# Output stages of the second network's mixers: where and when the split weights of output tiles 4, 5 and 7 are made

## The reference, cut to what matters

```python
for i in range(4):                       # mixers: gdn0, hgrn, gla, gdn1
    m = mixer_i(x, ...)                  # ends in o.reshape(B, T, 1024) @ w_out
    x = layer_norm(DN_ALPHA * x + m, mix_ln_g[i], mix_ln_b[i])
    x = layer_norm(DN_ALPHA * x + swiglu(x, ffn_w_in[i], ffn_w_down[i]), ...)
```

## Time and profile before

| what | value |
|---|---|
| device time, median of three | 2551.23 us (2549.55 to 2552.09) |
| span of the profiled execution | 2545.7 us |
| PE busy | 2464.1 us, 97% |
| DVE busy | 1769.0 us, 69% |
| ACT busy | 1179.2 us, 46% |
| granted PE clock over the 40 slices | 9 tenths or more in each |

### The profile page before, as it was taken

The page is one execution under the profiler, slowest core; times in us unless marked ns, Lnnn a source line. Parts: engine busy times, 40 slices in busy tenths (PEclk is TensorE's granted clock), DMA queues, the critical chain, the costliest instruction groups (busy, mean ns, idle before and its releaser), DMA issues.

```text
span 2545.7 us, 46612 instructions
## 1 busy us (share of the span) xinstructions
PE 2464.1 (97%) x17610; PEld 2261.9 (89%) x17610; DVE 1769.0 (69%) x2863; ACT 1179.2 (46%) x1816; POOL 105.9 (4%) x161
## 2 busy tenths in 40 slices
PE   8999999999999999989999999999989999989998
PEld 6866777778798999988999998999989999988997
DVE  5878699988747866675665767666457657766665
ACT  4554421223545444455544544544545446455443
POOL 2221000000000000003000000000000000000000
PEclk9999999999999999999999999999999999999999
DMA  7323255554424554321555431555415554222553
GB/s 296 141 104 137 100 182 186 183 182 154 167 92 148 191 181 162 112 84 67 173 182 189 159 108 67 181 181 183 157 51 177 186 179 152 100 75 75 198 178 121
DMA packets 119641, 378.13 MB, mean 149 GB/s; under 512 B 11592, under 2 KB 29000, under 8 KB 119121
## 3 DMA queue, kind: packets, MB, share of 16 engines
q1 hardware_dynamic: 105936, 327.58, 38.1%
q0 software_dynamic: 12528, 47.62, 5.4%
q10 hardware_dynamic: 1040, 1.05, 0.1%
HBM read 375.15 MB, written 1.05 MB: 148 GB/s over the span
## 4 chain that ended last, share of the span: by engine, by line
PE 85%; DVE 9%; ACT 4%; issue 2%; DMA 0%; DVEq 0%; ACTq 0%; SPq 0%
PE gb L597 22%; PE gb L598 21%; PE gb L599 21%; DVE w_lo L566 3%; PE mb L676 2%; PE mb L2636 2%; PE gb L1162 1%; ACT w_hi L560 1%; PE gb L2617 1%; PE gb L2132 1%; PE mb L2150 1%; PE mb L599 1%; PE mb L598 1%; PE mb L597 1%; DVE W L2372 1%
## 5 line engine op out<-in xcount | busy, mean ns | idle before, releaser
L597 PE MATMUL gb<-Xs,w_hi 128*128 128x256 f32 (+1 forms) x3584 | 1098.3, 306 | 18.1 <-DVE w_lo L566 5.2
L599 PE MATMUL gb<-Xs,w_lo 128*128 128x256 f32 (+1 forms) x3584 | 1083.3, 302 | 0.0
L598 PE MATMUL gb<-Xs,w_hi 128*128 128x256 f32 (+1 forms) x3504 | 1053.4, 301 | 0.0
L560 ACT ACTIVATE w_hi<-raw 128x1024 fp32r<-128x1024 f32 x616 | 646.6, 1057 | 775.8 <-PE gb L599 730.6
L566 DVE TENSOR_TENSOR w_lo<-raw,w_hi 128x1024 fp32r<-128x1024 f32 x616 | 747.7, 1225 | 222.6 <-ACT w_hi L560 215.6
L597 PEld LDWEIGHTS gb<-Xs,w_hi 128*128 128x128 f32 x3584 | 679.0, 189 | 73.6 <-issue 29.9
L599 PEld LDWEIGHTS gb<-Xs,w_lo 128*128 128x128 f32 x3584 | 678.5, 189 | 31.2
L598 PEld LDWEIGHTS gb<-Xs,w_hi 128*128 128x128 f32 x3504 | 664.3, 190 | 26.4 <-issue 1.2
L598 PE MATMUL gb<-Fs,w_hi 128*128 128x256 f32 (+1 forms) x1016 | 294.4, 290 | 0.0
L597 PE MATMUL gb<-Fs,w_hi 128*128 128x256 f32 (+1 forms) x936 | 263.2, 281 | 0.0
L599 PE MATMUL gb<-Fs,w_lo 128*128 128x256 f32 (+1 forms) x936 | 261.9, 280 | 0.0
(11 more groups left out here) (402 smaller groups left out, 2889.9 us busy)
## 6 DMA issues: line engine op xcount, KB each, us to landing
raw<-in_up SPq DMA_DIRECT2D x264, 512.0 KB, 3.8
raw<-in_down SPq DMA_DIRECT2D x96, 512.0 KB, 3.6
R<-in_mod_later POOLq DMA_DIRECT2D x80, 512.0 KB, 3.9
raw<-in_gdn_in SPq DMA_DIRECT2D x64, 512.0 KB, 3.6
raw<-in_down SPq DMA_DIRECT2D x48, 384.0 KB, 3.9
raw<-in_hgrn_in SPq DMA_DIRECT2D x32, 512.0 KB, 3.9
raw<-in_ev_in SPq DMA_DIRECT2D x24, 512.0 KB, 5.3
raw<-in_gla_in SPq DMA_DIRECT2D x24, 512.0 KB, 4.1
```

The lines of the kernel that those rows point to most:

```text
L560: nc.scalar.activation(w_hi[:, slot], raw[:, slot], ACT.Identity).then_inc(*hi_ready.inc())
L597: nc.tensor.matmul(to, w_hi[:, w_slot, k, :], x_hi, start=start, stop=False)
L598: nc.tensor.matmul(to, w_hi[:, w_slot, k, :], x_lo, start=False, stop=False)
L599: return nc.tensor.matmul(to, w_lo[:, w_slot, k, :], x_hi, start=False, stop=stop)
```

## The change

Output tiles 4, 5 and 7 of the four stages get places of their own for their split weights. Tile 4's and 5's lie in columns T to 2T of `Xs` (eight rows each), tile 7's in the first four rows of `R`, seen as `Rr`. `weights_at` and `weight_block` give the place, `Ahead.next` returns it beside the slot of `raw`, and `split_hi` no longer waits for `gemm_out` where the target is such a place. `act_out` takes the place of `act_squares` and `dve_out` that of `dve_residual` in these four stages: the order of splits against residual sums and squares is another. `SP`'s loads, the slots of `raw` and PE's order of matmuls are as before. The other stages with `pe_out`, `act_squares` or `dve_residual` keep their order.

```diff
--- before.py
+++ after.py
@@ -168,6 +168,8 @@
             pass
         X = sb("X", [P, KC, 2 * T])
         M = sb("M", [P, KC, T])
+        with nc.sbuf_tensor("Rr", [P, 4, KC, P], F32R) as Rr:
+            pass
         R = sb("R", [P, 8, 512])
         W = sb("W", [P, 8, 512])
         VC, NV = vector_columns()
@@ -357,6 +359,25 @@
                 runs[-1] += n
             kinds += [kind] * n
 
+        first_of = {name: sum(p[1] for p in plan[:j]) for j, (name, _, _) in enumerate(plan)}
+        aside_of = {}
+        OUT_ASIDE = {4: SLOTS + 3, 5: SLOTS + 4, 7: SLOTS}
+        aside_of.update({first_of[f"{mixer}_out"] + t: w for mixer in ("gdn0", "hgrn", "gla", "gdn1") if f"{mixer}_out" in first_of for t, w in OUT_ASIDE.items()})
+        pairs = lambda z: z.rearrange("p (r b) n -> p r b n", b=2)
+
+        def weights_at(w, part):
+
+            if w < SLOTS:
+                return (w_hi, w_lo)[part][:, w]
+            if w < SLOTS + 2:
+                return Rr[:, 2 * (w - SLOTS) + part]
+            r = 8 * (w - SLOTS - 3) + 4 * part
+            return Xs[:, r:r + 4, T:2 * T].rearrange("p r (b n) -> p r b n", b=2)
+
+        def weight_block(w, part, k):
+            z = weights_at(w, part)
+            return z[:, k, :] if len(z.shape) == 3 else z[:, k // 2, k % 2, :]
+
         @block.sync
         def _(sp):
             def mod_pair(g):
@@ -541,6 +562,8 @@
             def next(self):
 
                 slot = (self.at + self.n) % SLOTS if self.left > self.n else None
+                if slot is not None:
+                    slot = slot, aside_of.get(self.at + self.n, slot)
                 self.at += 1
                 self.left -= 1
                 return slot
@@ -554,16 +577,20 @@
         def split_hi(act, slot, fresh=False):
             if slot is None:
                 return
+            slot, to = slot if isinstance(slot, tuple) else (slot, slot)
             act.wait_ge(*loaded[slot].due("act", 16))
-            if not fresh:
+            if not fresh and to < SLOTS:
                 act.wait_ge(*gemm_out.seen("act"))
-            nc.scalar.activation(w_hi[:, slot], raw[:, slot], ACT.Identity).then_inc(*hi_ready.inc())
+            hi = weights_at(to, 0)
+            nc.scalar.activation(hi, raw[:, slot, 0:hi.shape[1]] if len(hi.shape) == 3 else pairs(raw[:, slot]), ACT.Identity).then_inc(*hi_ready.inc())
 
         def split_lo(dve, slot):
             if slot is None:
                 return
+            slot, to = slot if isinstance(slot, tuple) else (slot, slot)
             dve.wait_ge(*hi_ready.due("dve"))
-            nc.vector.tensor_tensor(w_lo[:, slot], raw[:, slot], w_hi[:, slot], ALU.subtract).then_inc(*lo_ready.inc())
+            hi, lo = weights_at(to, 0), weights_at(to, 1)
+            nc.vector.tensor_tensor(lo, raw[:, slot, 0:hi.shape[1]] if len(hi.shape) == 3 else pairs(raw[:, slot]), hi, ALU.subtract).then_inc(*lo_ready.inc())
 
         act_counts = ((hi_ready, "sent", BANKS), *((loaded[s], "act", 16) for s in range(SLOTS)), (gemm_out, "act", BANKS),
                       (gemm_taken, "act", BANKS))
@@ -594,9 +621,9 @@
 
 
         def pe_block(to, w_slot, k, x_hi, x_lo, start, stop):
-            nc.tensor.matmul(to, w_hi[:, w_slot, k, :], x_hi, start=start, stop=False)
-            nc.tensor.matmul(to, w_hi[:, w_slot, k, :], x_lo, start=False, stop=False)
-            return nc.tensor.matmul(to, w_lo[:, w_slot, k, :], x_hi, start=False, stop=stop)
+            nc.tensor.matmul(to, weight_block(w_slot, 0, k), x_hi, start=start, stop=False)
+            nc.tensor.matmul(to, weight_block(w_slot, 0, k), x_lo, start=False, stop=False)
+            return nc.tensor.matmul(to, weight_block(w_slot, 1, k), x_hi, start=False, stop=stop)
 
         def rows_of(k, n):
 
@@ -675,14 +702,14 @@
             for _ in range(n):
                 nc.tensor.matmul(mb[:, 0, :], ones[:, :], vec[:, 0:512], start=True, stop=True)
 
-        def pe_out(pe, n, ready, layer_norm=False, warm=5, order=tuple(range(KC)), rows=rows_of):
+        def pe_out(pe, n, ready, layer_norm=False, warm=5, order=tuple(range(KC)), rows=rows_of, aside={}):
 
             pe_group(pe, 0, n, ready, order, rows)
             for m in range(AHEAD, KC):
                 pe.wait_ge(*lo_ready.due("pe"))
                 pe.wait_ge(*gemm_taken.free("pe"))
                 for k in range(KC):
-                    last = pe_block(gb[:, m % BANKS, 0:n], m % SLOTS, k, *rows(k, n), k == 0, k == KC - 1)
+                    last = pe_block(gb[:, m % BANKS, 0:n], aside.get(m, m % SLOTS), k, *rows(k, n), k == 0, k == KC - 1)
                 last.then_inc(*gemm_out.inc())
             pe_stats(pe, n, layer_norm)
             pe_warm(pe, warm)
@@ -784,6 +811,21 @@
                     act_tile(act, 1)
             sq_added.due("act")
 
+        def act_out(act):
+
+            use_table(LN_EXP)
+            for _ in range(2):
+                split_hi(act, ahead["act"].next())
+            for m in range(KC):
+                gemm_out.due("act")
+                act.wait_ge(*gemm_taken.due("act"))
+                if m > 2:
+                    act.wait_ge(*sq_added.due("act"))
+                nc.scalar.activation(squares_at(m, T) if m else sq_sum(T), X[:, m, 0:T], ACT.Square, scale=1 / 32).then_inc(*sq_ready.inc())
+                for _ in range({2: 2, 3: 2, 6: 1, 7: 1}.get(m, 0)):
+                    split_hi(act, ahead["act"].next())
+            sq_added.due("act")
+
         def normed_tile(m, n):
             return W[:, 4 + m % 4, :] if n > T else work[:, m, :]
 
@@ -900,6 +942,18 @@
                 if layer_norm:
                     dve.wait_ge(*x_added.sent())
                 nc.vector.memset(small[:, 156:157], 0.0).then_inc(*sums_kept.inc())
+
+        def dve_out(dve):
+
+            dve_tile(dve, 3)
+            for m in range(KC):
+                dve.wait_ge(*gemm_out.due("dve"))
+                gemm_taken.due("dve")
+                nc.vector.scalar_tensor_tensor(out=X[:, m, 0:T], in0=X[:, m, 0:T], scalar=DN_ALPHA, in1=gb[:, m % BANKS, 0:T],
+                                               op0=ALU.mult, op1=ALU.add).then_inc(*gemm_taken.inc())
+                dve_sums(dve, m, T, True)
+                if 2 <= m < KC - 1:
+                    dve_tile(dve)
 
         def dve_residual(dve, layer, part, n, tiles, beside=None, stats=0, banks=None):
 
@@ -2200,7 +2254,7 @@
                 if g:
                     gn_sums(pe, (g - 1,), start=False)
             gn_sums(pe, (3,), start=False)
-            pe_out(pe, T, lambda k: None if k % 2 else pe.wait_ge(*gn_applied.due("pe")), layer_norm=True)
+            pe_out(pe, T, lambda k: None if k % 2 else pe.wait_ge(*gn_applied.due("pe")), layer_norm=True, aside=OUT_ASIDE)
 
         inv_base = {"pe": 0}
 
@@ -2929,7 +2983,7 @@
             for i, mixer in second:
                 if f"{mixer}_in" in names:
                     {"hgrn": act_hgrn, "gla": act_gla}.get(mixer, lambda e: act_gdn(e, i // 3))(act)
-                    act_squares(act, T, 1)
+                    act_out(act)
                     act_ln(act, "mix", i)
                 if f"up_2_{i}" in names:
                     act_ffn(act, None, T)
@@ -2974,7 +3028,7 @@
             for i, mixer in second:
                 if f"{mixer}_in" in names:
                     {"hgrn": dve_hgrn, "gla": dve_gla}.get(mixer, lambda e: dve_gdn(e, i // 3))(dve)
-                    dve_residual(dve, None, 0, T, 1, stats=T)
+                    dve_out(dve)
                     dve_ln(dve)
                 if f"up_2_{i}" in names:
                     dve_ffn(dve, None, T)
```

## The result

The changed kernel takes 2543.69 us (median of 20 runs, 2539.44 to 2550.35), the kernel before 2549.51 us (20 runs, 2542.99 to 2552.09). The ratio is 0.9980, 95% interval 0.9973 to 0.9986: 5.8 us between the medians, 3.6 to 6.9 us by the interval. Forecast were 2544.4 us, a gain of 6.8 us. Single runs of either kernel are spread over 9 to 11 us, more than the three runs shown of before let me think. A run's device time is 1.7 us longer than its span (2542.61 against 2540.9 us in the profiled run here); the 5.5 us that I put around a span of before was mostly this spread.

The account below looks back on a forecast made before the run. PE bounds the kernel, but DVE's fixed list limits the end of the four output stages. 3.9 us in three stages plus 2.9 in gdn0 make 6.8 off the median of 2551.23: 2544.4 us, range 2542.5 to 2546.

Parts of the forecast that it names:

- What bounds: Four output stages: PE stands waiting for DVE, whose fixed list of splits and residual sums limits the stage's end.
- The early splits: Two splits each on DVE and ACT fit the idle before the first residual sum; in gdn0 that sum is 0.05 late.
- The new wait: DVE's splits of tile 6 and n2 wait for ACT's: a step of 3.01 us, not 2.45, twice per stage.
- Three stages at 1.3 us each: hgrn, gla and gdn1: line 669 and all behind it start 1.3 us sooner, 3.9 us in all.
- gdn0 at 2.9: gdn0's output stage: 2.28 us from an earlier line 669 plus 0.6 from the clock; bounds 2.2 and 4.9.
- the 0.11 that I added for the running sums: gdn0's waiting steps: 0.11 us each for what POOL costs the running sums, within 3.38 us per step.
- The clock: gdn0's statistics: shorter PE gaps keep the full clock, saving 0.6 us on lines 669 and 671.
- PE reading its weights from elsewhere: PE's matmuls of tiles 4, 5 and 7, with weights from `Xs` and `R`: taken as nothing, at most 5 us a stage.
- most of the gain lost in the wait: Rival, chance 0.20: DVE's last sum comes late; with 1 us lost per stage the gain is 2.8, 2548.4 us.
- The rival that ended slower: Chance 0.05: weights from `Xs` slow matmuls of tiles 4 and 5 to 0.189 us; 5.7 us slower, 2556.9.
- Its turning point: Slower weights from `Xs` turn the change into a loss from about 0.035 us per matmul on.
- The larger gain: Rival, chance 0.10: DVE early enough everywhere; 4.9 us in gdn0, 1.4 in each other stage, 9.1 in all, 2542.1.

Follow-up runs that it names:

- e1: The changed kernel with the split of n2 again behind the residual sum of tile 7; ratio 0.9975 to the kernel before.
- e2: The changed kernel with DVE back in its old order, ACT's early splits and the new places kept; 2544.68 us, executed once.
- e4: The changed kernel with POOL's signal to build its tables given behind gdn0's layer norm, not ahead of gdn0's output stage; 2539.90 us, executed once.
- e8: The changed kernel with tile 7 in its slot as before, ACT splitting it after the square of m = 3; 2547.99 us, executed once.

## Why the prediction was right

*What bounds.* Right: in three stages DVE's list, up to the point where PE takes over; in gdn0 DVE throughout. e1 separates the two, and e2 shows that the gain comes from DVE's list: with ACT's early splits and DVE's old order, 0.34 of hgrn's 1.45 us are left.

*The early splits.* They fit: the first sum is not later anywhere, not even in gdn0 (7.98). The new places cost nothing on the engines that write them, as the earlier trace rows had it:

```profile
L593 DVE TENSOR_TENSOR w_lo<-raw,w_hi x604: 1149/1220/1482, 38.2 to 2520.4; 128x1024 fp32r<-128x1024 f32 x151
L593 DVE TENSOR_TENSOR Xs<-raw,Xs x8: 1218/1220/1311, 1186.9 to 2318.3; 128x1024 fp32r<-128x1024 f32 x8
L593 DVE TENSOR_TENSOR Rr<-raw,Rr x4: 1218/1219/1486, 1196.0 to 2326.0; 128x1024 fp32r<-128x1024 f32 x4
```

*The new wait.* The step that I put at 3.01 us is 1573.21 - 1570.21 = 3.00 and 1583.67 - 1580.67 = 3.00. The last sum of hgrn, forecast 23.27 after the start (1582.38 - 1559.11), came at 23.03. Most of the difference lies in the first three sums, which take 1.59 us from the first to the third and not 1.85. The second follows at 0.34, not at 0.42. The third follows at 1.25: the 1.43 that I took was the last step of the list, in which DVE also waits for the running sums ahead of the memset.

*Three stages at 1.3 us each.* They gave 1.45, 1.38 and 1.33, together 4.2 for 3.9. X tile 7's product gained 1.57 and not 1.24, since back-to-back matmuls overlap more than I allowed. 0.13 of it goes back behind it: the product of its square (698) must now wait for ACT, and the warming products start 0.99 after 696 instead of 0.86.

*gdn0 at 2.9.* It gave 2.68, and that this is so near is luck: two terms were mis-sized and a third left out, and they cancel. The product of X tile 7 gained 3.18 instead of 2.28: the waiting steps took 3.00 and 2.99, not 3.38. DVE's split was 1.23 long there instead of the 1.48 I took over from the earlier trace rows, and the 0.11 that I added for the running sums ran beside ACT's split. The clock gave 0.51 (1.49 to 0.98 from that product to the warming products) for my 0.6. And 1.01 us were given back in the layer norm, 4.20 to 5.21 us from the first warming product to the next stage, which the prediction said would simply move along. Before, POOL was done at 1206.3, when the layer norm began, 29.2 us after the stage's start; now the norm begins 3.55 us sooner in the stage, and POOL is done 30.4 us after its start. e4 shows the cause of three quarters of it: with POOL moved, DVE's three centring steps are back at 1.08 us, and from there to the first tile of `Xs` it takes 2.69 us, as before the change, against 3.44 in the changed kernel.

The Trainium skill, "SBUF — State Buffer", section "Who interferes with whom", has a DVE instruction with two inputs in SBUF contend with a GpSimd instruction that reads SBUF, for a shared pair of ports that is an exclusive lock. The trace agrees that they disturb one another (splits of 1.48 us beside POOL, 1.22 without), and shows that a split can also get through at 1.23.

*PE reading its weights from elsewhere.* Rightly at nothing: the last of the 192 matmuls starts 22.51 to 22.63 us after the first, 22.37 to 22.58 before. The loads of weights from `Xs` and from `Rr`, which the prediction had no row for:

```profile
L624 PEld LDWEIGHTS gb<-Xs x64: 187/192/192, 1192.9 to 2328.7; 128*128 128x128 f32 x64
L624 PEld LDWEIGHTS gb<-Xs,Rr x32: 187/188/189, 1201.5 to 2334.3; 128*128 128x128 f32 x32
```

The median load from `Xs` takes 192 ns, from `Rr` 188, as from `w_hi`, and the matmuls don't come later for it. The rival that ended slower is out. Its turning point of 0.035 us per matmul was worked out wrong: at 0.035 the three stages lose 1.1 us together while gdn0, whose end is DVE's, still gains 2.9; by the prediction's own terms the loss begins at 0.04 or a little above.

*The rivals.* The first, most of the gain lost in the wait, was real in mechanism: the waits cost 0.55 each (3.00 against 2.45). They stood in my sum already, and e8 shows what one more would have cost, 0.58. The larger gain did come in the three stages, 4.16 us for its 3 x 1.4, but not in gdn0, where 2.68 came and it wanted 4.9.

*The total.* 6.8 forecast, 6.84 in the stages, 5.1 by the ratio (3.6 to 6.9), 5.8 between the medians. That 2543.69 lies within 0.7 us of 2544.4 is luck in part: the kernel before came out 1.7 us lower than the 2551.23 that I subtracted from. What nobody could read from one profile is the spread of executions ahead of the stages, several us. Against the 5.1 us (0.2%) I gave as the bound, the gain was nearer to being lost in it than the stage lengths suggest.

## What to carry to other kernels

Where one engine works off a fixed list while another waits for its last entry, count the list's entries and look for the idle stretch before its first: entries moved there, if they have somewhere to write, leave the stretch that counts (here that brought 1.11 of hgrn's 1.45 us). Price the new neighbours too: a two-engine hand-over (ACT's half, then DVE's) put into one step of the list costs a wait each time, here 0.55 us (3.00 against 2.45), and a step ahead it costs nothing. And compare kernels by the length of the stage from mark to mark, which came back within 0.03 us in the one repetition, not by the span of one execution, which differed by 2 us for other reasons.

## What the runs showed of the hardware

The disturbance of DVE by POOL is not a rate: splits beside POOL take from 1.22 to 1.49 us, and which one is hit changes with the timing. POOL pays in turn. Where n2's split got through at 1.23 us (from 1204.61), POOL's instruction that began behind it took 1.37 us; the next one of its line took 0.32:

```profile
1204.65 1.37 POOL L471 TENSOR_TENSOR Xr<-X 128x64 fp32r<-128x64 f32 x1
1205.98 0.32 POOL L471 TENSOR_TENSOR Xr<-X,tri 128x64 fp32r<-128x64 f32 x1
```

The split of 1.49 us (1195.95 in the changed kernel) met one of POOL's that had begun before it, at 1195.75. The residual sums, with one of their two inputs in `gb`, took 0.41 to 0.42 us in gdn0 as elsewhere. The disturbance also moves along a kernel: shortening one engine's list shifted it from the sums into the layer norm.

PE's clock, 0.54 on average after 3.14 us of idle time in the earlier trace rows, stayed at 1.00 with 0.67 us, as it did with 1.24 us in the earlier trace rows. In e2's gdn0 stage it fell after an idle time of 2.26 us, to the lower level, 1.2 GHz. The first line is the product of line 692, the second the stretch from it to the warming products:

```profile
1201.29 0.94 PE L692 MATMUL mb<-W,ones 128*128 128x256 f32 x2 [2.26 <-DVE small L944]
...
1201.20:1204.60 3.40, 3.31 (x9) 2.67 (x10) 2.09 (x5) 1.61 (x3) 3.10 (x7) 0.56 0.57 196
```

It did not fall within the idle time: there it was granted at 1.00 (1200.0 to 1201.2), then 0.70 in the us in which PE took up work again, and 0.50 from 1202.2 to 1204.6.
